# V of both mixers in chunks of 512 rows by 512 columns instead of 1024 rows by 256 columns

## The reference

```
# first block
h = rms_norm(x, norm_mix_pre)
proj = h @ w_in                       # q, k, v (12 heads of 128 each), GLU input, gates
a = dilated_attention(q, k, v, rel_bias)
y_a = a @ w_attn_out
c = silu(layer_norm(causal_depthwise_conv(c_val * sigmoid(c_gate))))
x = x + rms_norm((g_a * y_a + g_c * (c @ conv_pw_w)) @ w_out)
x = x + rms_norm(conv-FFN(x))
# second block
x = x + 0.5 * swiglu(...)
p = rms_norm(x) @ w_in_2              # RWKV columns, then q, k, v (8 heads of 64) and f of FoX, gates
x = x + (gate_a * (rwkv7_mixer(p) @ rwkv_proj) + gate_b * (fox_mixer(p) @ fox_proj)) @ w_out_2
x = x + 0.5 * swiglu(...)
```

## Time and profile before

| | us |
|---|---|
| median of three runs | 1264.79 (1262.45 to 1265.44) |
| the profiled execution | 1261.77 |
| its span, first to last instruction | 1260.0 |
| TensorE busy (matmul) | 1202.5 |
| mean granted TensorE clock | 0.965 of full speed |

### The profile page before, as it was taken

The page is one execution under the profiler, slowest core; times in us unless marked ns, Lnnn a source line. Parts: engine busy times, 40 slices in busy tenths (PEclk is TensorE's granted clock), DMA queues, the critical chain, the costliest instruction groups (busy, mean ns, idle before and its releaser), DMA issues. The chain is left out here.

```text
span 1260.0 us, 24434 instructions
## 1 busy us (share of the span) xinstructions
PE 1202.5 (95%) x10783; PEld 1175.6 (93%) x10783; DVE 775.5 (62%) x1056; ACT 552.4 (44%) x614; POOL 154.6 (12%) x113
## 2 busy tenths in 40 slices
PE   6999999989899999899999989999899989999998
PEld 5999999989899999899999987989888789999998
DVE  3588976747587677655554567864257564645453
ACT  4433345473365454453434355422333445434343
POOL 3888770000000000000000000012000000000000
PEclk9999999999799999989999997999999989999999
DMA  6567553345155555526555543323032333655640
GB/s 210 167 220 250 171 170 127 112 156 175 39 192 176 200 168 179 187 67 201 184 164 185 178 155 101 115 89 102 3 101 100 114 121 101 200 188 180 200 167 34
DMA packets 143602, 187.48 MB, mean 149 GB/s; under 512 B 4368, under 2 KB 128841, under 8 KB 143517
## 3 DMA queue, kind: packets, MB, share of 16 engines
q1 hardware_dynamic: 142173, 182.70, 44.6%
q0 software_dynamic: 1104, 3.49, 0.8%
q10 hardware_dynamic: 240, 0.06, 0.0%
HBM read 185.17 MB, written 2.64 MB: 149 GB/s over the span
## 5 line engine op out<-in xcount | busy, mean ns | idle before, releaser
L1900 PE MATMUL bank<-X_hi,w_hi 128*128 128x256 f32 x1968 | 572.3, 291 | 17.1 <-DVE X_lo L1560 11.7
L1901 PE MATMUL bank<-X_lo,w_hi 128*128 128x256 f32 x1968 | 567.1, 288 | 0.0
L1902 PE MATMUL bank<-X_hi,w_lo 128*128 128x256 f32 x1968 | 566.6, 288 | 0.0
L1900 PEld LDWEIGHTS bank<-X_hi,w_hi 128*128 128x128 f32 x1968 | 387.1, 197 | 22.4 <-issue 16.0
L1290 ACT ACTIVATE w_hi<-w_raw 128x2048 fp32r<-128x2048 f32 x172 | 328.3, 1910 | 181.2 <-PE bank L1902 172.5
L1901 PEld LDWEIGHTS bank<-X_lo,w_hi 128*128 128x128 f32 x1968 | 387.6, 197 | 0.0
L1902 PEld LDWEIGHTS bank<-X_hi,w_lo 128*128 128x128 f32 x1968 | 387.0, 197 | 0.0
L1538 DVE TENSOR_TENSOR w_lo<-w_raw,w_hi 128x2048 fp32r<-128x2048 f32 x146 | 333.7, 2286 | 84.8 <-ACT w_hi L1290 84.6
L1900 PE MATMUL bank<-Y_hi,w_hi 128*128 128x256 f32 x656 | 187.8, 286 | 2.3 <-DVE Y_lo L1103 1.4
L1901 PE MATMUL bank<-Y_lo,w_hi 128*128 128x256 f32 x656 | 186.9, 285 | 0.0
L1902 PE MATMUL bank<-Y_hi,w_lo 128*128 128x256 f32 x656 | 186.8, 285 | 0.0
(11 more groups left out here) (268 smaller groups left out, 1045.2 us busy)
## 6 DMA issues: line engine op xcount, KB each, us to landing
w_raw<-in_ffn_w_dram SPq DMA_DIRECT2D x66, 1024.0 KB, 5.4
w_raw<-in_w_in_dram SPq DMA_DIRECT2D x54, 1024.0 KB, 5.2
w_raw<-in_w_up_dram SPq DMA_DIRECT2D x22, 1024.0 KB, 5.1
w_raw<-in_w_down_dram SPq DMA_DIRECT2D x11, 1024.0 KB, 4.9
w_raw<-in_w_out_dram SPq DMA_DIRECT2D x8, 1024.0 KB, 4.9
w_raw<-in_conv_pw_w_dram SPq DMA_DIRECT2D x4, 1024.0 KB, 4.9
w_raw<-in_w_attn_out_dram SPq DMA_DIRECT2D x2, 1024.0 KB, 4.9
w_raw<-in_rwkv_proj_dram SPq DMA_DIRECT2D x2, 1024.0 KB, 4.9
```

The costliest lines, as they stand in the source:

```text
L1900: pe.matmul(o, wh, xh, start=start, stop=False, skip_group_check=True)
L1901: pe.matmul(o, wh, xl, start=False, stop=False, skip_group_check=True)
L1902: return pe.matmul(o, wl, xh, start=False, stop=stop, skip_group_check=True)
```

## The change

Both weights' V columns are cut differently. A pair of chunks now covers 512 columns: the first has rows 0 to 511, the second rows 512 to 1023. The count of chunks, their size of 1 MB and the total of loads stay. `by_tokens` takes the half kh: for 4 row tiles and 2 token tiles it issues three matmuls with 512 moving columns, 24 to a chunk. A pair fills two banks, one for each 128 tokens, and both banks are complete only at the end of its second chunk. TensorE waits for both banks at the start of the pair. ScalarE reads them after the pair with two activations of 128 x 512; in the second block this is at the start of n = 4 alone. The pairs of the first block take banks (2, 0), (1, 2) and (0, 1).

```diff
+        def wide_chunk(w, kh, c0):
+            return w[0, kh * 512:(kh + 1) * 512, c0:c0 + 512].rearrange("(k p) c -> p k c", p=P)
...
-        for j in range(3 * QKV // 256):
+        for j in range(2 * QKV // 256):
             add((col_chunk(w_in, 256 * j), 0))
+        for j in range(QKV // 512):
+            for kh in range(2):
+                add((wide_chunk(w_in, kh, 2 * QKV + 512 * j), 0))
...
-        for j in range(6):
+        for j in range(4):
             add((col_chunk(w_in_2, SHIFT + 256 * j), 0))
+        for kh in range(2):
+            add((wide_chunk(w_in_2, kh, SHIFT + 1024), 0))
...
-                if n < 4:
-                    columns(B_FOX + 2 + n, tokens=n >= 2)
+                if n == 1:
+                    columns(B_FOX + 3)
+                if n == 2:
+                    for t in range(TT):
+                        pe.wait_ge(S[f"bank{bank_of[B_FOX + 4 + t]}_read"], reads[B_FOX + 4 + t] - 1)
+                if n in (2, 3):
+                    by_tokens(B_FOX + 2 + n, n - 2)
...
-            def v_tokens(j):
-
-                m = B_FOX + 4 + j
-                act.wait_ge(S["chunk_used"], m + 1)
-                v = [a.activation(fv[:, t, 256 * j:256 * j + 256], bank[bank_of[m]][:, t * T:t * T + T],
-                                  ACT.Copy, scale=rcol[:, t:t + 1]) for t in range(TT)]
...
+            def v_tokens():
+
+                act.wait_ge(S["chunk_used"], B_FOX + 6)
+                for t in range(TT):
+                    b = bank_of[B_FOX + 4 + t]
+                    a.activation(fv[:, t, :], bank[b][:, :], ACT.Copy, scale=rcol[:, t:t + 1]).then_inc(
+                        S[f"bank{b}_read"], 1)
...
-                if n in (3, 4):
-                    v_tokens(n - 3)
+                if n == 4:
+                    v_tokens()
...
-                    j = n - A_QKV - 12
-                    act.wait_ge(S["chunk_used"], n + 1)
...
+                    j, kh = divmod(n - A_QKV - 12, 2)
+                    if kh:
+                        act.wait_ge(S["chunk_used"], n + 1)
+                        for t in range(TT):
+                            b = bank_of[n - 1 + t]
+                            a.activation(v_t[:, t, 512 * j:512 * j + 512], bank[b][:, :], ACT.Copy,
+                                         scale=rcol[:, t:t + 1]).then_inc(S[f"bank{b}_read"], 1)
...
-            def by_tokens(n, slot, b):
+            def by_tokens(n, kh):
+
 
                 split_ready(n)
-                for k in range(NT):
-                    wh, wl = (w[slot][:, k * 256:k * 256 + 256] for w in (w_hi, w_lo))
+                slot = n % RING
+                for k in range(4):
+                    wh, wl = (w[slot][:, k * 512:k * 512 + 512] for w in (w_hi, w_lo))
                     for t in range(TT):
-                        xh, xl = (h[:, k, t * P:(t + 1) * P] for h in (X_hi, X_lo))
-                        mm = three(bank[b][:, t * T:t * T + T], (xh, xl), (wh, wl), start=k == 0 and t == 0,
-                                   stop=k == NT - 1)
+                        xh, xl = (h[:, 4 * kh + k, t * P:(t + 1) * P] for h in (X_hi, X_lo))
+                        o = bank[bank_of[n - kh + t]][:, :]
+                        first, last = kh == 0 and k == 0, kh == 1 and k == 3
+                        pe.matmul(o, xh, wh, start=first, stop=False, skip_group_check=True)
+                        pe.matmul(o, xl, wh, start=False, stop=False, skip_group_check=True)
+                        mm = pe.matmul(o, xh, wl, start=False, stop=last, skip_group_check=True)
...
-                if reads[n] - 1 > 0:
-                    pe.wait_ge(S[f"bank{b}_read"], reads[n] - 1)
+                kh = max(n - A_QKV, 0) % 2
+                for m in ([n] if n < A_QKV + 12 else [n, n + 1] if kh == 0 else []):
+                    if reads[m] - 1 > 0:
+                        pe.wait_ge(S[f"bank{bank_of[m]}_read"], reads[m] - 1)
...
-                    by_tokens(n, n % RING, b)
+                    by_tokens(n, kh)
```

More of the change, by code:

```diff
@@ L421, in pe_mixer, with columns @@
         def pe_mixer(told, pe, state, by_columns, by_tokens, by_rows, sum_squares, spread):
-            def columns(n, fresh=False, tokens=False, midway=None):
+            def columns(n, fresh=False, midway=None):
                 pe.wait_ge(S[f"bank{bank_of[n]}_read"], reads[n] - 1)
-                if tokens:
-                    by_tokens(n, n % RING, bank_of[n])
-                else:
-                    by_columns(n, n % RING, bank_of[n], fresh=fresh, midway=midway)
+                by_columns(n, n % RING, bank_of[n], fresh=fresh, midway=midway)
             def to_tokens(src, c, t, h, o):
@@ L759, in act_mixer @@
             copies("x_first", 1, x_inv, 6, "x_copied")
-            def v_tokens(j):
-                m = B_FOX + 4 + j
-                act.wait_ge(S["chunk_used"], m + 1)
-                v = [a.activation(fv[:, t, 256 * j:256 * j + 256], bank[bank_of[m]][:, t * T:t * T + T],
-                                  ACT.Copy, scale=rcol[:, t:t + 1]) for t in range(TT)]
-                v[0].then_inc(S["v_half"], 1)
-                v[1].then_inc(S[f"bank{bank_of[m]}_read"], 1)
+            def v_tokens():
[4 more added lines that the diff above has]
+                        S[f"bank{b}_read"], 1)
             for n in range(1, LEVELS + 1):
-                if n in (3, 4):
-                    v_tokens(n - 3)
+                if n == 4:
+                    v_tokens()
                 for f in range(2):
@@ L1416, in _ @@
                 if n >= A_QKV + 12:
-                    j = n - A_QKV - 12
-                    act.wait_ge(S["chunk_used"], n + 1)
-                    v = [a.activation(v_t[:, t, 256 * j:256 * j + 256], bank[n % 3][:, 256 * t:256 * t + 256],
-                                      ACT.Copy, scale=rcol[:, t:t + 1]) for t in range(TT)]
-                    v[0].then_inc(S["v_half"], 1)
-                    v[1].then_inc(S[f"bank{n % 3}_read"], 1)
+                    j, kh = divmod(n - A_QKV - 12, 2)
[5 more added lines that the diff above has]
+                                         scale=rcol[:, t:t + 1]).then_inc(S[f"bank{b}_read"], 1)
             def exps(it):
```

## The result

| | before | after |
|---|---|---|
| median, runs taken together on one chip (16 and 16) | 1264.16 us (1262.18 to 1265.8) | 1265.96 us (1263.95 to 1268.99) |
| the profiled execution | 1261.77 | 1267.08 |
| its span | 1260.0 | 1265.3 |
| mean granted clock | 0.965 | 0.960 |

The ratio is 1.0018 [1.0011, 1.0026], some 2.3 us slower. The forecast was 2.0 us faster. One execution of `before_fill32` ran in a much slower state (1662.0 us) and is left out of its row in the table of experiments.

What follows compares the result with a forecast made beforehand. TensorE, 95% busy, was taken to bound the kernel by its matmul pace in V. 144 p - 33.07 at p = 0.216 gave -0.81 - 1.15 = -2.0 us, so 1264.8 becomes 1262.8 us; 8 in 10: 1259.0 to 1266.4.

Steps and rivals of the forecast that it cites:

- No idle time, full clock; what the matmuls cost counts: Both V stretches: TensorE never idle, at 2.4 GHz, so matmul pace counts; a chunk of 5.76 us becomes 5.18.
- The pace p = 0.216: Wide V matmuls start 0.216 us apart, the load hidden beneath; bounds 0.213 and 0.240, zero gain at 0.230.
- First block, 96p - 21.55: First block's change in us for pace p, through ScalarE's delivery of chunk 26 and VectorE's chain: 0.81 us gained.
- Second block, 48(p - 0.240): Second block's change in us for pace p: two chunks save 0.58 each, 1.15 us gained, ScalarE's later read hidden.
- Nothing else is late there: Second block: its two chunks stand between products without a gap, so their whole 1.15 us gain arrives.
- at nothing: GpSimd's `w_lo` and the reshaped weight loads cost nothing; half a microsecond for a chunk if the load slack were gone.
- What would show it: Signs against, in the V chunks: pace 0.23 or more, first-block clock under 1.00, or a `w_lo` wait there.
- The first: Rival on V's wide matmuls: width brings nothing, p near 0.240, +1.5 us, 1266.3; chance 0.08.
- The second: Rival: gaps between the first block's pairs lower the clock, 1.7 us each, +1.4 in all, 1266.2; chance 0.07.
- The third: Rival: first block's gain eaten by a longer read or VectorE slip; only second block's -1.15 stays, 1263.6; chance 0.13.
- the fourth: Rival: half-clock stretches elsewhere fall otherwise; two fewer -5.4 us, 1259.4, chance 0.13; two more 1266.2, chance 0.03.
- The fifth: Rival: V's columns run faster than one per cycle, together about -12 us, 1253; chance 0.01.

Runs made afterwards that it cites:

- before_fill32: Kernel before plus 32 identity products of 64 x 64, on alternating array halves, ahead of `lora_landed` in the second block; 1264.01 us, ratio 1.0016.
- widths: Changed kernel with the first block's pair 1 as 384 + 128 columns, pair 2 as four times 128, pair 3 as 512; 1277.79 us, one run.
- halves: Changed kernel with each 512-column matmul cut into two of 256, same order, banks and waits; 1263.77 us, ratio 1.0013.
- second_only: Kernel before with only the second block's V changed to the wide form; 1261.85 us, ratio 0.9993.
- bank3_both: Changed kernel, both blocks wide, first block's pairs in banks (3, 0), (1, 2), (3, 0), `w_hi` of chunk 26 made earlier, no filler; 1265.68 us, ratio 1.0018.
- after_again: The changed kernel itself, timed and profiled again; 1265.99 us, ratio 1.0026 against the kernel before.
- bank3_first: Changed kernel with only the first block wide, its pairs in banks (3, 0), (1, 2), (3, 0), `w_hi` of chunk 26 earlier; 1259.55 us, ratio 0.9968.
- fill64: Changed kernel plus 64 identity products of 64 x 64, on alternating array halves, ahead of `lora_landed` in the second block; 1262.56 us, ratio 0.9993.
- fill32: Changed kernel plus 32 identity products of 64 x 64, on alternating array halves, ahead of `lora_landed` in the second block; 1261.52 us, ratio 0.9979.
- bank3_fill32: Kernel of `bank3_both` plus 32 identity products, all in one place of the array, ahead of `lora_landed` in the second block; 1264.24 us, ratio 1.0000.
- pad32: Changed kernel plus 32 identity products of 64 x 64 at TensorE's start, into a bank nobody reads then; 1264.01 us, ratio 1.0008.

## Why the prediction was wrong

- **"No idle time, full clock; what the matmuls cost counts"**: right. Every chunk's saving was found at once in the starts.
- **The pace p = 0.216**: wrong size. It is 0.227, inside the bounds of 0.213 to 0.240 and near the decision point of 0.230. The value was taken from the nearest row, which is of another format; the row of the very format had already shown 0.013 above the columns' time, and `widths` shows that this part stays. The step from "something else of about 0.12 us", taken for the load, to "the load hides beneath" was the false one. The Trainium skill's 2.5 ns ("TensorE: Matmul & The Clock Gate", Back-to-back issue gap) is a fixed part too, but here it is 13 ns; its 131 ns at 512 columns was not seen in any run.
- **First block, 96p - 21.55**: the mechanism was right. With the measured pace it gives 96 x 0.227 - 21.55 = +0.24, and +0.25 to +0.26 were measured. The bank waits (1.05 forecast, 0.99 measured), the two reads of 1.28 (1.27) and VectorE's chain as the path (start 168.64 with the later start of V, no gap in it) all came as worked out. `halves` has the waits without the width: +1.44.
- **Second block, 48(p - 0.240)**: with 0.227 it is -0.62, and `second_only` shows -0.55. ScalarE's later read was hidden, as said.
- **"Nothing else is late there"**: this is the step that failed. The sum of the two blocks' terms at the measured pace is +0.26 - 0.55 = -0.3 us, within what can't be measured. The kernel came out 2.3 slower, and the 1.3 to 2.9 us by which the second block of `bank3_both`, `after_again` and after is longer than that of `second_only` are a term that the sum didn't have: the change removes one and a half blocks of code, and TensorE runs out of instructions among its fastest products. The list of what each edit costs counted engines, queues, banks and loads, but never the instructions themselves. The loads of weights stood "at nothing" because TensorE waits for none of them; by the times above they can still cost, by holding up a packet of code.
- **"What would show it"**: none of the three signs that were to make the forecast wrong appeared (the pace was 0.227, the clock 1.00 among the six chunks, and no `w_lo` was waited for), and it was wrong all the same, by something that the list didn't have. Of what was to confirm it, only the idle time before chunks 22 and 24 came (0.8 us each).
- **Rivals.** The first (width brings nothing) is false, though a chunk gains only 0.31 us of the 0.58. The second (gaps lower the clock) is false where it was put: 1.00 in all six chunks. But its mechanism came behind the new gap, and not always: in after's profile 3.4 us at half clock followed it (second block 34.23), in `after_again` none (32.83). The third is close to what the first block did; the fourth can't be separated from scatter in a single profile: behind the start of the recurrence before has 24.0 us at half clock, `bank3_first` 22.3, and `before_again`, the unchanged kernel, 22.3 too. The fifth is false.

**What stays open.** The local terms don't add up to the totals. `bank3_first` shows 1.94 us in its segment and is 4 faster; `bank3_both` differs from it locally by 0.7 and in total by 6. Of the kernels with the gap, after, `after_again`, `before_fill32` and `bank3_both` (which has 2 us in hand from its first block) are at 1.0016 to 1.0026, but `fill64` is at 0.9993. `fill32` differs from `after_again` by 0.8 in its segment and by 0.5% in the ratio. So the gap is shown, that the place of the code makes it is shown, and its local price is shown (1.3 to 1.55 from start to start, and up to 1.4 more with the clock); that it is the whole of the loss is only argued. The profile of `after_again` has the gap and a span of 1257.1 us, below that of before (1260.0). The mean granted clock over all runs is lower in after (0.9598), `after_again` (0.9600) and `bank3_both` (0.9586) than in before (0.961 to 0.962), but `fill64` (0.9632) and `before_fill32` (0.9618) have the gap without that, and `second_only` (0.9603) and `bank3_fill32` (0.9602) have the lower clock without the gap. Within one kernel a run whose mean clock is lower by 0.001 is 0.6 us longer, an estimate from the 246 runs of the four sessions. With the clock taken out in this way, the mean differences to before are +1.0 in `after_again`, 0.0 in `fill64`, -0.1 in `bank3_both` and +1.0 in `before_fill32`, where the segments give +1.2, +1.2, -1.2 and +1.3. So half-clock stretches elsewhere carry a part, and over 1 us of two of these kernels stays open. No profile shows why the clock differs.

## What to carry to other kernels

Before pricing a wider matmul, fit the pace of its own format to columns plus a fixed part at both clocks, and don't take the excess at a small width for a load that will hide. A change that adds or removes instructions shifts all code behind it against blocks of 256; look for idle time "issue" inside loops of very short matmuls, see whether a large load runs when the code for them falls due, and repeat a surprising small result with half a block of harmless filler before believing it. A bank wait that a change brings in can be removed where a bank is idle in that stage; here that, with the earlier copy of weights, gave 2.2 us in the first block, and the width gave 1.2 (`halves` to after).

## What was unexpected of the hardware

- TensorE's supply of instructions can run dry: 64 x 64 products at 0.0303 us a record, which use up a block of 16384 bytes in 3.9 us, gaps of 0.2 to 1.44 us that depend on the position modulo 256 instructions. The packet around the third group of products starts within 0.5 us of the end of a load of 1 MB, in all 18 traces.
- fp32r matmuls with a load each: 0.112, 0.120, 0.173 and 0.227 us at 128, 256, 384 and 512 columns at full clock.
- The same 64 records of 64 x 64 took 7.09 us at the program's start (`pad32`) and 3.94 us ahead of `lora_landed` (`bank3_fill32`), both times in one place of the array, and 2.08 us when they alternated between its halves (`fill32`). The last two were at full clock. At the start the clock is not known: its first record in `pad32` is at 13.85 us, and the view shows 1.00 where there is none. In before it also shows 1.00 at 16 to 19 us, while matmuls of 256 columns follow every 0.21 us there, the pace of half clock. So the 7.09 are probably the half clock for the most part.
